# First attention of a two-layer block: keys on the partitions in place of turned probabilities

## The chip, the cores and the metric

The kernel runs on one core of one Trainium2 chip. The metric is the device time of one execution in microseconds; lower is better.

## The reference, cut to what matters

Two blocks run one after the other on 2048 tokens of width 1024. The change touches only the attention of the first, which has 4 heads, keys of 128 + 64 features (the 64 are rotated and shared by the heads) and values of 128:

```python
s = (jnp.einsum('bqhd,bkhd->bhqk', qn, k_nope)
     + jnp.einsum('bqhr,bkr->bhqk', qr, k_rope)).astype(jnp.float32) * scale
mask = pq[:, None, :, None] >= positions[:, None, None, :]
p = jax.nn.softmax(jnp.where(mask, s, neg), axis=-1)
return jnp.einsum('bhqk,bkhd->bqhd', p.astype(v.dtype), v)
```

The result times silu(gate_a), beside a pooling branch times silu(gate_b), goes through `w_out` and a layer norm. All is float32. Every query meets all 2048 keys; those after it are masked by position, not skipped.

## The kernel before

The first block works with features on the partitions and tokens as columns, in G = 4 groups of TB = 512 tokens. It begins with keys and values of all groups. Then each group g goes through three parts: the query tiles (`query_tiles`, L112: latents, gate_a, pool inputs, queries, gate_b, pool mix), the attention (`mla_steps`, L72) and the eight tiles of the out-projection (`("1out", g, c)`). The layer norm of group g - 1 runs inside the query tiles of group g. The second block follows, and the change leaves it as it is.

The order of the work is one list, `schedule()`. Each name in it is a PSUM tile; tiles go round RING = 6 banks. TensorE claims a tile after the reader of the tile six before has drained it (`claim`, L1845), and its readers wait with `wait_tile` (L699) and `wait_drained` (L702). Two more banks, `o_acc`, hold the value sums. Weight chunks of 512 KB pass through four slots in the order of the list (`stream_of`, L430): the queue of SP waits for a chunk's last tile and then loads the chunk four on. SP also loads the next group's x, before the weights of the first out-projection tile (L811 to L816). A project (L1853) is eight matmuls of 128 x 128 by 512 columns. A float32 matmul leaves two records in the trace, a transpose of 128 x 128 one.

The attention of a group works on units (`mla_units`, L67): two blocks of 128 queries of one head, eight units per group. In a unit TensorE computes scores with queries on the partitions: per block four tiles of 128 queries by 512 keys (k_nope, L1961), then the 64 rotated features (L1965), which use half the rows of the array, two matmuls side by side. VectorE drains each tile with `tensor_tensor_reduce` (L1397): it adds a bfloat16 mask made once per block (`mask_of`, L1344) and keeps the running maximum of each row. Two tiny instructions (L1406, L1407) give the negated maximum, and one instruction of ScalarE exponentiates 2048 columns with the maximum as bias and leaves the row sum (L1068). Now queries are on the partitions, and values need keys there. So TensorE turns the probabilities in blocks (L1977), ScalarE copies them out of PSUM (L1061), and TensorE multiplies values by them, 256 columns per matmul, into `o_acc` (L1987). The scores of the next unit are interleaved with the turns and values of this one. After every second unit VectorE takes the reciprocal of four sums, widens it (L1416), TensorE turns it (L1996), and VectorE multiplies it by gate and `o_acc` into `y_all` (L1422, L1426), on which the out-projection waits. GpSimd has no instruction in this part. Three buffers of probabilities rotate: two halves of `probs` and `lat` (L534).

Other lines that the steps touch: L1354 and L1355 normalise the query latents, L1379 multiplies the pooled branch by its gate, L1339 normalises key latents of 1024 columns, L880, L943, L944, L948 and L959 are GpSimd's, L1649 and L1650 VectorE's beside them in the second block, L1781 its drain of second-attention scores. L1890 makes keys.

Of the kernel before, what the change touches and what calls it, by code (L numbers as in the profile page):

```python
# [7 lines left out]
S = 2048  # L8
# [25 lines left out]
HUGE = 3e38  # L34

# [28 lines left out]
TILES_1 = S // TB  # L64


def mla_units(g):  # L67

    return [(BG * g + b, h) for b in range(0, BG, 2) for h in range(H1)]


def mla_steps(g):  # L72

    units = mla_units(g)

    def scores(u, e):
        return [("score", u, e), ("exp", u, e)] if u < len(units) else []

    yield from scores(0, 0) + scores(0, 1)
    for u, (i, h) in enumerate(units):  # L80
        first, second = scores(u + 1, 0), scores(u + 1, 1)
        yield from first[:1]
        yield from [("turn", u, c) for c in range(2)]
        yield from first[1:]
        yield ("value", u, 0)
        if h % 2 == 0 and u > 0:
            yield from [("share", u - 1), ("blend", u - 1)]
# [5 lines left out]
        if h % 2 == 1:  # L93
            yield ("sums", u)
        yield from [("value", u, c) for c in range(TILES_1 - 2, TILES_1)]
    yield from [("share", u), ("blend", u)]


def mla_tiles(g):

    units = mla_units(g)
    for st in mla_steps(g):
        i, h = units[st[1]]
        if st[0] == "score":
            yield from [("score", i + st[2], h, c) for c in range(TILES_1)]
        elif st[0] == "turn":
            yield from [("prob_t", i + e, h, st[2]) for e in range(2)]
        elif st[0] == "share":
            yield ("share1_t", i, h // 2)


def query_tiles(g):  # L112
# [10 lines left out]
    yield from [("gate_a", g, j) for j in range(2, 4)]  # L123
# [321 lines left out]
def program(nc, A, out_t):  # L445
# [10 lines left out]
    with ctx:  # L456
# [38 lines left out]
        mask = alloc(one, "mask", [P, 2, S], bf16)  # L495
# [38 lines left out]
        probs_1 = probs[:, 0:S], probs[:, S:2 * S], lat[:, :, :].rearrange("p j t -> p (j t)")  # L534
        turned_1 = [a.rearrange("p e t -> p (e t)") for a in (prob_t[:, 0:2, :], turns[:, :, :])]
# [39 lines left out]
        def y_of(g):  # L575
            return y_all

# [53 lines left out]
        row_max = sem("row_max")  # L631
# [85 lines left out]
        def half_units_before(g, u, e):  # L717

            return 2 * (len(mla_units(0)) * g + u) + e

        def blends_before(g, u):

            return (len(mla_units(0)) * g + u) // 2
# [69 lines left out]
        def _(sp):  # L793
# [8 lines left out]
            for name, arr, idx, _ in STREAM:  # L802
# [8 lines left out]
                if name[0] == "1out" and name[2] == 0 and name[1] + 1 < G:  # L811
                    if name[1] == 0:
                        wait_tile(sp, "krope", G - 1)
                    else:
                        sp.wait_ge(stored, 16 * name[1])
                    load_x(name[1] + 1, A["x_t"])  # L816
# [43 lines left out]
        def _(pool):  # L860
# [38 lines left out]
            for g in range(G):  # L899
# [20 lines left out]
                for j in range(4):  # L920
                    ins = pool.tensor_copy(halo[:, j, :], u_in[:, j, TB:TB + HALO])
                    step(pool, ins)
            pool.wait_ge(win_summed, 4 * G)
# [40 lines left out]
        def _(act):  # L964
# [61 lines left out]
            for g in range(G):  # L1026
# [7 lines left out]
                for j in range(4):  # L1034
# [14 lines left out]
                units = mla_units(g)  # L1049
                for st in mla_steps(g):  # L1050
                    kind, u = st[:2]
                    i, h = units[u]
                    if kind == "turn":
                        c = st[2]
                        m = (len(units) * g + u) * TILES_1 + c
                        to = turned_1[m % 2].rearrange("p (k e q) -> p k e q", k=BG, e=2)
                        for e in range(2):
                            wait_tile(act, "prob_t", i + e, h, c)
                            if m >= 2 and e == 0:
                                act.wait_ge(pv_done, m - 1)  # L1060
# [1293 lines left out]
```

## Time and profile before

| what | value |
|---|---|
| median of 3 runs | 3818.19 us (3817.41 to 3819.34) |
| the profiled execution | 3818.23 us |
| its span | 3816.4 us |
| mean granted TensorE clock | 0.964 of full speed |
| TensorE busy | 3511.4 us |
| VectorE, ScalarE, GpSimd busy | 1800.6, 1434.4, 415.0 us |

The span is the time from the first to the last record of the profiled execution. Busy times are sums over one engine's instructions, so engines that work side by side add to more than the span. The granted clock is 1.00 at 2.4 GHz and 0.50 at 1.2 GHz.

### The profile page before, as it was taken

To read this page: it belongs to the slowest core of one execution; us is meant where nothing else is said; L and a number is where in the kernel's file an instruction comes from. 1 tells how busy PE (TensorE), PEld (TensorE's weight loads), DVE (VectorE), ACT (ScalarE), POOL (GpSimd) and SP (SyncE) were. 2 spreads that over 40 slices of the span, in tenths; PEclk is the share of its full clock that TensorE was granted. 3 is DMA by queue.
4 is the path that set the end of the run, shared out by engine and by line. 5 is a ranking of instruction groups with operands and counts; after the bars stand their busy time and mean duration, and the time that the engine had idled before them with its cause. 6 is when DMAs were issued, how large, how long until landed. Compare 5 with 4: busy or idle time off the path is not lost.

```text
span 3816.4 us, 38713 instructions
## 1 busy us (share of the span) xinstructions
PE 3511.4 (92%) x14032; PEld 1921.9 (50%) x14032; DVE 1800.6 (47%) x4239; ACT 1434.4 (38%) x2445; POOL 415.0 (11%) x445
## 2 busy tenths in 40 slices
PE   8999999999999999999979989899897898787887
PEld 3445644564456446645545445654445643444653
DVE  3413322332232323234662577825778616878652
ACT  1213312341233114222331465515665515766551
POOL 0001011002100210011111201202011111010100
PEclk9999999999999999989989999899998999898999
DMA  4121013002300220041103121031110031110002
GB/s 175 55 83 39 1 61 121 12 1 72 121 1 6 77 89 1 28 149 63 60 9 113 61 67 37 23 99 55 61 42 1 23 113 44 47 53 1 1 8 82
DMA packets 71885, 205.55 MB, mean 54 GB/s; under 512 B 6376, under 2 KB 7952, under 8 KB 71440
## 3 DMA queue, kind: packets, MB, share of 16 engines
q1 hardware_dynamic: 63360, 187.32, 15.3%
q10 hardware_dynamic: 8336, 15.74, 1.1%
q8 instruction: 114, 1.87, 0.2%
q14 instruction: 75, 0.61, 0.0%
HBM read 185.46 MB, written 17.58 MB: 53 GB/s over the span
## 4 chain that ended last, share of the span: by engine, by line
PE 73%; DVE 12%; ACT 8%; issue 5%; DMA 1%; SPq 0%; POOL 0%; ACTq 0%; DVEq 0%; POOLq 0%
PE bank L1859 37%; PE bank L1961 6%; PE o_acc L1987 6%; PE bank L1965 3%; PE bank L1977 3%; PE bank L2199 3%; PE bank L2084 3%; PE bank L2211 2%; ACT prob_t L1123 2%; PE bank L2116 2%; PE o_acc L2225 2%; ACT pt_last L1123 1%; DVE rstd L1519 1%; PE bank L2065 1%; DVE tmp L1571 1%
## 5 line engine op out<-in xcount | busy, mean ns | idle before, releaser
L1859 PE MATMUL bank<-group_even,weights 128*128 128x512 f32 x1376 | 601.5, 595 | 17.1 <-DMA weights<-in_w_in_kv 11.7
L1859 PE MATMUL bank<-group_odd,weights 128*128 128x512 f32 x1376 | 607.8, 599 | 6.2 <-ACT tmp L1109 6.2
L1859 PE MATMUL bank<-y_all,weights 128*128 128x512 f32 x1024 | 441.6, 593 | 12.9 <-DVE y_all L1426 6.0
L1859 PEld LDWEIGHTS bank<-group_even,weights 128*128 128x128 f32 x1376 | 260.7, 191 | 337.0 <-issue 336.9
L1859 PEld LDWEIGHTS bank<-group_odd,weights 128*128 128x128 f32 x1376 | 262.9, 193 | 331.6 <-issue 331.3
L1859 PEld LDWEIGHTS bank<-y_all,weights 128*128 128x128 f32 x1024 | 193.9, 190 | 255.8 <-issue 241.1
L1397 DVE CUSTOM_DVE_ANT_0 probs<-bank,mask 128x512 f32<-128x512 f32 x172 | 108.5, 687 | 261.9 <-PE bank L1965 261.9
L1961 PE MATMUL bank<-k_nope,q_nope 128*128 128x512 f32 x512 | 231.1, 594 | 0.0
L2199 PE MATMUL bank<-kh,qa 64*128 64x512 f32 (+3 forms) x816 | 175.0, 501 | 31.0 <-DVE mx L1781 18.7
L1250 ACT ACTIVATE prob_t<-bank 128x512 f32<-128x512 f32 (+3 forms) x240 | 116.7, 535 | 148.6 <-PE bank L2211 148.3
L2225 PE MATMUL o_acc<-prob_t,v 128*64 128x128 f32 x1680 | 148.7, 285 | 11.1 <-ACT prob_t L1250 7.3
L1068 ACT ACTIVATE probs<-probs,stat 128x2048 f32<-128x2048 f32 x43 | 86.5, 2012 | 171.2 <-DVE stat L1407 171.2
L2225 PEld LDWEIGHTS o_acc<-prob_t,v 128*64 128x64 f32 x1680 | 120.7, 141 | 57.7 <-issue 40.9
L1961 PEld LDWEIGHTS bank<-k_nope,q_nope 128*128 128x128 f32 x512 | 94.4, 190 | 101.1 <-issue 99.8
L1315 DVE TENSOR_TENSOR tmp<-bank,turns 128x512 f32<-128x512 f32 x12 | 8.3, 692 | 252.7 <-PE bank L1859 249.8
L1965 PE MATMUL bank<-k_rope,q_rope 64*128 64x512 f32 x512 | 127.2, 615 | 0.0
L1987 PE MATMUL o_acc<-prob_t,val 128*128 128x256 f32 x512 | 126.3, 389 | 0.0
L2199 PEld LDWEIGHTS bank<-kh,qa 64*128 64x128 f32 x816 | 81.1, 197 | 88.5 <-issue 37.8
L1061 ACT ACTIVATE prob_t<-bank 128x512 f32<-128x512 f32 x128 | 70.1, 600 | 140.1 <-PE bank L1977 139.2
L1123 ACT ACTIVATE prob_t<-index,mids 128x384 bf16<-128x384 f32 (+2 forms) x72 | 64.7, 898 | 152.3 <-DVE mids L1592 142.5
L1987 PE MATMUL o_acc<-turns,val 128*128 128x256 f32 x512 | 121.0, 379 | 0.0
L730 DVE SCALAR_TENSOR_TENSOR group_even<-group_even,bank 128x512 f32<-128x512 f32 x32 | 22.0, 686 | 202.5 <-PE bank L1859 202.5
(386 smaller groups left out, 5564.2 us busy)
## 6 DMA issues: line engine op xcount, KB each, us to landing
weights<-in_w_in SPq DMA_DIRECT2D x101, 512.0 KB, 3.5
weights<-in_w_in_q SPq DMA_DIRECT2D x64, 512.0 KB, 3.5
weights<-in_w_out SPq DMA_DIRECT2D x64, 512.0 KB, 3.6
weights<-in_w_i SPq DMA_DIRECT2D x20, 512.0 KB, 3.5
group_even<-in_x_t SPq DMA_DIRECT2D x8, 1024.0 KB, 8.0
group_odd<-in_x_t SPq DMA_DIRECT2D x8, 1024.0 KB, 8.8
group_even<-x_t SPq DMA_DIRECT2D x8, 1024.0 KB, 8.3
group_odd<-x_t SPq DMA_DIRECT2D x8, 1024.0 KB, 7.2
```

The costliest lines, as they stand in the source:

```text
L1068: A_(p, p, ACT.Exp, scale=QK_DIM ** -0.5, bias=stat[:, 8 + n % 3:9 + n % 3], accum_out=stat[:, 16 + 2 * h + e:17 + 2 * h + e]).then_inc(pr ...
L1123: A_(tested_act[m % 2][:, 0:share], index_of(BG * g + b)[:, n - share:n], ACT.Sign, scale=-1.0, bias=mids[:, b, r:r + 1], accum_out=signs[ ...
L1250: drains(A_(prob_slots[2 * (m % 2) + e][:, 0:wide_], bank("p2_t", i, 2 * p + e, c)[:, 0:wide_], ACT.Copy), "p2_t", i, 2 * p + e, c)
L1397: drains(V.tensor_tensor_reduce(out=probs_1[n % 3][:, c * TB:(c + 1) * TB], in0=bank("score", i + e, h, c)[:], in1=mask[:, e, c * TB:(c + ...
L1859: ins = M(bank(*name)[:], ring[n % SLOTS][:, k * P:(k + 1) * P], rhs[:, k, :], start=(k == 0), stop=(k == chunks - 1))
L1961: M(bank("score", i + e, h, c)[:], q_nope[:, h, cols], k_nope[:, h, c * TB:(c + 1) * TB], start=True, stop=False)
L1965: M(bank("score", i + e, h, c)[:], q_rope[half, h, cols], k_rope[half, (c // 2) * TB:(c // 2 + 1) * TB], start=False, stop=True).then_inc( ...
L1977: ins = nc.tensor.transpose(bank(*name)[:, k * P:(k + 1) * P], probs_1[n % 3][:, at:at + P], ident[:])
L1987: ins = M(o_acc[h // 2][:, (h % 2) * 2 * P:(h % 2 + 1) * 2 * P], val[:, c * BG + k, h * P:(h + 1) * P], turned_1[m % 2][:, 2 * k * P:2 * ( ...
L2084: ins = M(bank(*st)[:], x_of(g)[:, k, b * P:(b + 1) * P], w[:, (k % 2) * TB:(k % 2 + 1) * TB], start=(k == 0), stop=(k == KC - 1))
L2199: ins = M(bank("s2", i, 2 * p + e, c)[:, at:at + end - first], qa[rows, p, (i % BG) * P:(i % BG + 1) * P], kh[rows, a, p, first:end], star ...
L2225: ins = M(o_acc[i % 2][e * DH2:(e + 1) * DH2, p * P:(p + 1) * P], v2[:, k, h * DH2:(h + 1) * DH2], prob_slots[2 * (m % 2) + e][:, (k % BG) ...
```

## The change

Scores come with keys on the partitions: the key block is the stationary operand and 512 queries stream past it. Their exponentials can be multiplied with values as they are, and nothing is turned but three rows of maxima and shares per head. A unit is now a head with all 512 queries, four per group; it has eight pairs of tiles, each tile 128 keys by 512 queries. A step s of `mla_steps` does the scores of pair s and the values of pair s - 10 (`LAG`).

- VectorE drains a score tile with one instruction: the minimum of the score and (query position + 0.5 - key position) times 2 to the 80.
- The maximum of a query is now over partitions. VectorE takes an elementwise running maximum of pairs, folds it, TensorE turns it (peak), VectorE reduces, ScalarE widens, TensorE turns it back (spread), ScalarE copies it to `peaks`.
- The peaks are subtracted from each pair in place, by GpSimd for pairs 2 and 5 of each head and by VectorE for the rest; ScalarE exponentiates pairs of 1024 columns.
- Sums over keys: GpSimd adds the pairs 0 to 6 of a head elementwise (0 to 3 in the last head of a group), VectorE the rest and the two parts together, during the steps of the head after the next (total); TensorE multiplies them with ones (sums), and a share is widened, turned and multiplied as before, once per head.
- Twelve slots of pairs rotate: `probs`, `lat`, `turns`, the buffer of the next x and a quarter of `y_all`. So the next x is loaded only after the first tile of the out-projection.
- The projections gate_a 2 and 3 move from the query tiles into the attention. gate_a 3 is copied raw, its silu follows near the end.
- Each out-projection tile takes the chunks 4 to 7 first, then 0 to 3, and its first tile waits for the last head only at chunk 3.

```diff
-        for c in range(2, TILES_1):
-            yield ("turn", u, c)
-            if c < TILES_1 - 1:
-                yield ("value", u, c - 1)
-        yield from second
+PAIRS_1 = NB // 2
+LAG = 10
+KEY_SLOTS = 12
+POOL_SHIFTS = (2, 5)
+def key_tiles(p):
+    a, j = p // BG, p % BG
+    return [(2 * a + e) * BG + j for e in range(2)]
+def sums_by_pool(u):
+    return 7 if u < H1 - 1 else 4
+def mla_steps(g):
+    total = H1 * PAIRS_1
+    for s in range(total):
+        u, p = s // PAIRS_1, s % PAIRS_1
+        yield ("score", s)
+        if s == PAIRS_1:
+            yield from [("peak", 0), ("gate_a", 2), ("spread", 0)]
+        elif u > 0 and p == 0:
+            yield ("peak", u - 1)
+        elif u > 1 and p == 1:
+            yield ("spread", u - 1)
+        if s >= LAG:
+            yield ("value", s - LAG)
+        if s >= LAG - 1:
+            yield ("shift", s - LAG + 1)
+        if u > 1 and p in (1, 2, 3):
+            yield ({1: "total", 2: "sums", 3: "share"}[p], u - 2)
+    u = H1 - 1
+    v = total - PAIRS_1
+    yield from [("shift", v - 1), ("value", v - 2), ("peak", u), ("value", v - 1), ("spread", u), ("total", u - 1), ("gate_a", 3),
+                ("sums", u - 1), ("shift", v), ("shift", v + 1), ("value", v)]
+    for n in range(v + 1, total):
+        if n + 1 < total:
+            yield ("shift", n + 1)
+        if n == v + 2:
+            yield ("share", u - 1)
+        if n == total - 1:
+            yield from [("total", u), ("sums", u)]
+        yield ("value", n)
+    yield ("share", u)
...
# SP: when the next x is loaded
-                if name[0] == "1out" and name[2] == 0 and name[1] + 1 < G:
+                if name[0] == "1out" and name[2] == SLOTS and name[1] + 1 < G:
...
# GpSimd
+                    if kind == "shift" and p in POOL_SHIFTS:
+                        pool.tensor_tensor(tiles, tiles, peaks[u % 2].unsqueeze(1).broadcast_to([P, 2, TB]),
+                                           ALU.subtract).then_inc(shifted_pool, 1)
+                    elif kind == "value" and p < sums_by_pool(u):
+                        pool.wait_ge(probs_made, pairs_before(g, n) + 1)
...
+                            sum_of(pool, pool.tensor_tensor(sum_pool, sum_pool, tiles[:, 0, :], ALU.add))
+                            pool.tensor_tensor(sum_pool, sum_pool, tiles[:, 1, :], ALU.add).then_inc(far_sum, 1)
...
# ScalarE
+                        A_(tiles, tiles, ACT.Exp, scale=QK_DIM ** -0.5).then_inc(probs_made, 1)
...
# VectorE
+                            drains(V.scalar_tensor_tensor(out=tiles[:, e, :], in0=query_pos, scalar=pos_q[:, t:t + 1],
+                                                          in1=bank("score", g, n, e)[:], op0=ALU.subtract, op1=ALU.min), "score", g, n, e)
...
+                            step(dve, V.tensor_tensor(lane_max2, lane_max2, tiles, ALU.max))
+                        if p == PAIRS_1 - 1:
+                            V.tensor_tensor(max_dve, lane_max2[:, 0, :], lane_max2[:, 1, :], ALU.max).then_inc(lane_max, 1)
...
+                        V.tensor_tensor(tiles, tiles, wide(peaks[u % 2], 2), ALU.subtract).then_inc(shifted, 1)
...
# TensorE
+                        for e, t in enumerate(key_tiles(p)):
+                            M(bank("score", g, n, e)[:], k_nope[:, h, t * P:(t + 1) * P], q_nope[:, h, :], start=True, stop=False)
+                        at = p * P
+                        for e in range(2):
+                            half = slice(e * ROPE, (e + 1) * ROPE)
+                            M(bank("score", g, n, e)[:], k_rope[half, at:at + P], q_rope[half, h, :],
+                              start=False, stop=True).then_inc(tile_ready, 1)
...
+                        pe.wait_ge(probs_made, pairs_before(g, n) + 1)
+                        for e, t in enumerate(key_tiles(p)):
+                            ins = M(o_acc[h % 2][:], val[:, t, h * P:(h + 1) * P], key_slot(g, n)[:, e, :],
+                                    start=(p == 0 and e == 0), stop=(p == PAIRS_1 - 1 and e == 1))
```

## Rows read from the trace of the kernel before

**Rows 1.** the page's busy time, share of the span and instructions.

```profile
PE 3511.4 (92%) x14032; PEld 1921.9 (50%) x14032; DVE 1800.6 (47%) x4239; ACT 1434.4 (38%) x2445; POOL 415.0 (11%) x445
```

**Rows 2.** busy time, clock and DMA by stretch: the first attention stage.

```profile
core 0: us, PE busy (x) PEld busy (x) DVE busy (x) ACT busy (x) POOL busy (x), PEclk, DMA share, GB/s
...
312.20:489.50 177.30, 175.40 (x786) 111.37 (x784) 58.81 (x182) 67.39 (x97) 0.00 (x0) 1.00 0.00 1
```

**Rows 3.** timeline of TensorE over one unit (start us, length us).

```profile
379.71 3.60 PE L1961 MATMUL bank<-k_nope,q_nope 128*128 128x512 f32 x8
...
388.72 3.60 PE L1961 MATMUL bank<-k_nope,q_nope 128*128 128x512 f32 x8
392.24 1.99 PE L1965 MATMUL bank<-k_rope,q_rope 64*128 64x512 f32 x8
394.16 1.97 PE L1977 MATMUL bank<-ident,probs 128*128 128x128 f32 x16
396.09 1.97 PE L1987 MATMUL o_acc<-prob_t,val 128*128 128x256 f32 x8
...
401.36 3.17 PE L1961 MATMUL bank<-k_nope,q_nope 128*128 128x512 f32 x7
```

**Rows 4.** query normalisation on VectorE and its reader on TensorE, group 1 (timeline).

```profile
584.92 2.29 DVE L1355 TENSOR_TENSOR lat<-lat,rstd 128x2048 f32<-128x2048 f32 x1
...
629.47 20.76 PE L1859 MATMUL bank<-lat,weights 128*128 128x512 f32 x48
```

**Rows 5.** groups on VectorE, 150 to 500 us (busy us, mean ns | idle).

```profile
L1397 DVE CUSTOM_DVE_ANT_0 probs<-bank,mask 128x512 f32<-128x512 f32 x44 | 27.8, 687 | 67.6 <-PE bank L1965 67.6
...
L1379 DVE SCALAR_TENSOR_TENSOR y_all<-bank,vec,y_all 128x512 f32<-128x512 f32 x4 | 3.0, 750 | 4.7 <-PE bank L1944 4.4
...
L1339 DVE TENSOR_TENSOR lat<-lat,rstd 128x1024 f32<-128x1024 f32 x1 | 1.2, 1225 | 0.0
```

**Rows 6.** groups on ScalarE from 300 to 500 us.

```profile
L1068 ACT ACTIVATE probs<-probs,stat 128x2048 f32<-128x2048 f32 x11 | 22.1, 2011 | 47.6 <-DVE stat L1407 47.6
L1061 ACT ACTIVATE prob_t<-bank 128x512 f32<-128x512 f32 x32 | 17.5, 598 | 35.0 <-PE bank L1977 34.8
```

**Rows 7.** timeline of VectorE, its start after the rope matmuls of rows 3.

```profile
393.54 0.69 DVE L1397 CUSTOM_DVE_ANT_0 lat<-bank,mask 128x512 f32<-128x512 f32 x1 [4.82 <-PE bank L1965]
```

**Rows 8.** GpSimd: seven additions in a chain (timeline), and 1024 columns (groups).

```profile
575.45 9.34 POOL L880 TENSOR_TENSOR probs<-probs 128x512 f32<-128x512 f32 x7 [0.42 <-ACT probs L1011]
...
L948 POOL TENSOR_TENSOR y_all<-probs 128x1024 f32<-128x1024 f32 x8 | 15.1, 1893 | 129.1 <-DVE probs L1650 129.1
```

**Rows 9.** GpSimd, VectorE in the second block (timelines from 3385 us); L943's group.

```profile
3385.48 1.42 POOL L943 TENSOR_TENSOR y_all<-probs 128x512 f32<-128x512 f32 x1 [7.62 <-DVE probs L1650]
3386.87 1.54 POOL L944 TENSOR_TENSOR y_all<-probs 128x512 f32<-128x512 f32 x1
...
3385.32 0.69 DVE L1649 TENSOR_TENSOR kh<-kh,probs 128x512 f32<-128x512 f32 x1
3386.04 1.41 DVE L1650 TENSOR_TENSOR kh<-kh,probs 128x512 f32<-128x512 f32 x1
...
L943 POOL TENSOR_TENSOR kh<-probs 128x512 f32<-128x512 f32 x24 | 24.9, 1039 | 75.5 <-DVE kh L1650 75.5
```

**Rows 10.** GpSimd and VectorE with a PSUM operand, from 2403 us (timelines).

```profile
2403.43 4.52 POOL L959 TENSOR_TENSOR group_odd<-bias,sel 128x256 f32<-128x256 f32 x7
...
2404.21 0.42 DVE L1781 CUSTOM_DVE_ANT_0 index<-bank,group_odd 128x256 f32<-128x256 f32 x1
```

**Rows 11.** TensorE at the end of the stage (timeline; in brackets idle time before).

```profile
489.46 11.00 PE L1859 MATMUL bank<-y_all,weights 128*128 128x512 f32 x25 [1.51 <-DVE y_all L1426]
```

**Rows 12.** TensorE after idle time (timeline); clock by stretch.

```profile
161.98 8.79 PE L1890 MATMUL bank<-lat,gate 128*128 128x512 f32 x16 [7.39 <-DVE lat L1339]
170.61 7.03 PE L1896 MATMUL bank<-gate,lat 128*128 128x512 f32 x16
...
154.00:162.00 8.00, 0.61 (x3) 0.02 (x1) 7.72 (x7) 0.69 (x1) 0.00 (x0) 0.78 0.16 61
```

More of the change, by code:

```diff
@@ L112, in query_tiles @@
+def mla_tiles(g):
+    for kind, n in mla_steps(g):
+        if kind == "score":
+            yield from [("score", g, n, e) for e in range(2)]
+        elif kind in ("peak", "spread", "sums", "share", "gate_a"):
+            yield ({"share": "share1_t", "sums": "sums1"}.get(kind, kind), g, n)
 def query_tiles(g):
@@ L122, in query_tiles @@
         yield ("1var", g - 1)
-    yield from [("gate_a", g, j) for j in range(2, 4)]
     yield from [("u", g, j) for j in range(4)]
@@ new lines, in widened @@
+                def widened(to, of):
+                    return A_(to.rearrange("p (b q) -> p b q", b=BG), of.unsqueeze(2).broadcast_to([P, BG, P]), ACT.Copy)
+                for kind, n in mla_steps(g):
+                    if kind == "peak":
+                        wait_drained(act, "peak", g, n)
+                        widened(tmp[:, 0, :], stat[:, 0:BG]).then_inc(peaks_wide, 1)
+                    elif kind == "spread":
+                        wait_tile(act, "spread", g, n)
+                        drains(A_(peaks[n % 2], bank("spread", g, n)[:], ACT.Copy), "spread", g, n)
+                    elif kind == "shift":
+                        u, p = n // PAIRS_1, n % PAIRS_1
+                        by_pool = units_before(g, u) * len(POOL_SHIFTS) + sum(q < p for q in POOL_SHIFTS)
+                        if p in POOL_SHIFTS:
+                            act.wait_ge(shifted_pool, by_pool + 1)
+                        else:
+                            act.wait_ge(shifted, pairs_before(g, n) - by_pool + 1)
+                        tiles = key_slot(g, n)
+                        A_(tiles, tiles, ACT.Exp, scale=QK_DIM ** -0.5).then_inc(probs_made, 1)
+                    elif kind == "gate_a":
+                        wait_tile(act, "gate_a", g, n)
+                        drains(A_(gate[:, n, :], bank("gate_a", g, n)[:], ACT.Silu if n < H1 - 1 else ACT.Copy), "gate_a", g, n)
+                    elif kind == "sums":
+                        if n == H1 - 1:
+                            wait_drained(act, "gate_a", g, n)
+                            A_(gate[:, n, :], gate[:, n, :], ACT.Silu).then_inc(gate1_made, 1)
+                        wait_drained(act, "sums1", g, n)
+                        widened(tmp[:, 1, :], stat[:, BG:2 * BG]).then_inc(shares1_made, 1)
@@ new lines, in _ @@
+                        for e in range(2):
+                            wait_drained(dve, "score", g, n, e)
+                        if p == 0:
+                            held_tiles = tiles
+                        elif p == 1:
+                            if units_before(g, u) > 0:
+                                before = units_before(g, u) - 1
+                                wait_tile(dve, "peak", before // H1, before % H1)
+                            step(dve, V.tensor_tensor(lane_max2, held_tiles, tiles, ALU.max))
+                        else:
+                            step(dve, V.tensor_tensor(lane_max2, lane_max2, tiles, ALU.max))
@@ L1928, in _ @@
                     variance_of("1", g - 1, sq_view(probs))
-                for j in range(2, 4):
-                    project(("gate_a", g, j), x_of(g), KC)
                 for j in range(4):
```

281 lines of the change are left out of this document (131 added, 150 removed).

## The prediction

> **What bounds the kernel now.** I read the engine summary first [rows 1]: TensorE is busy for 92% of the span and no other engine for half of it. Then the busy time by stretch [rows 2]: of each first-attention stage of 177.3 us (it comes four times, once per group of 512 queries) TensorE works 175.4 at a granted clock of 1.00, VectorE 58.8, ScalarE 67.4, GpSimd nothing. So the stage is TensorE's work in order, and any other engine has more than 100 us of room. TensorE's timeline [rows 3] gives that work for one unit (256 queries of one head): it starts at 379.71 and its successor at 401.36. Eight score tiles cost 2 x (3.53 + 1.92) = 10.9 us (start to start, 388.72 to 392.24 to 394.16). Sixteen of its 32 transposes take 1.93, so all take some 3.7, and 7.1 are left for the values. Eight units are 173.3 us, with four sets of share transposes and 1.9 us of idle time the 177.3. Per head and group (two units) that is 44.3 us. Only the transposes of probabilities, 8 x 3.7 = 29 us per stage, are work that another layout does without.
>
> **The change on TensorE.** A head of 512 queries now takes eight steps: two score tiles, then two value matmuls of the step ten back. Plain matmuls of 512 columns come at 0.43 us per record (48 in 20.76) [rows 4], 3.43 for eight where L1961 takes 3.53 before it changes to half rows [rows 3]. So two L1961 matmuls take 1.72 us and two value matmuls also 1.72. The rope pair is not halved in the same way. Before, four rope matmuls run two by two and take 1.92, of which 1.72 is streaming; 0.20 there and 0.10 at the end of L1961 are paid each time TensorE goes to half rows and back. Now it goes there for every pair: 1.72 + 0.10 + 0.86 + 0.20 = 2.88 per step instead of 2.73. A step is 2.88 + 1.72 = 4.60 us, 32 of them 147 us. Peak, spread and share turn four blocks each, 0.5 us at the 0.12 us per block of L1977 [rows 3]; the four one-column matmuls of sums are weight loads at best, eight records at that pace, 0.9. Together 2.4 per head, 9.5 per stage. gate_a 2 and 3 (sixteen records each, 2 x 6.87 us) move from the query tiles into the stage: TensorE's work is unchanged, and the cover they gave the query normalisation isn't needed, for L1355 ends at 587.2 and its reader starts at 629.5 [rows 4]. I therefore compare with 177.3 + 13.7 = 191.0. Pure TensorE work after is 147 + 9.5 + 13.7 = 170.5.
> The Trainium skill (TensorEngine Tiling (Array Packing), Key Properties) says that a change of tiling mode drains the engine; the trace agrees, with 0.30 us for a round trip. If switching cost nothing the step would be 4.30.
>
> **The new chain.** TensorE now waits in every step for something made a step ago. After the score pair of a step, VectorE drains two tiles (0.61 + 0.69, L1397's pitch and length [rows 5]), takes the maximum over 1024 columns (1.22, from L1339) and subtracts the peaks for the next pair (1.22); ScalarE then exponentiates 1024 columns, 1.07 between 0.60 for 512 and 2.01 for 2048 [rows 6]. VectorE starts 1.30 us after the rope matmuls start [rows 3, 7], 0.2 after TensorE could go on. With 0.15 for hand-overs that is 5.3 us from the end of a score pair to probabilities. TensorE wants them after 4.60. Since a late value also delays the next score, the pace is the mean of both, about 4.95.
> Two of eight subtractions are GpSimd's. It sits in an in-order queue behind the sum of the pair before, two additions of 1.26 to 1.35 (seven in 9.34) [rows 8]. Its 1024-column subtraction lies between 1.89 (L948, one operand a repeated column) and 2 x 1.26 = 2.52; I take 2.3.
>
> **VectorE and GpSimd together.** Before, GpSimd is idle in this stage. Where both run on SBUF operands later, the trace shows them excluding each other [rows 9]: GpSimd's L943 starts under L1649 and takes 1.42 instead of the 1.04 of its group; VectorE's L1650 starts under L943 and takes 1.41 instead of 0.69, ending 0.55 after L943 does; L944 in turn takes 1.54. An instruction of VectorE with one operand in PSUM doesn't show this: L1781 takes 0.42 beside L959, seven of which take 4.52 [rows 10]. So drains and share products are free; maxima, subtractions and sums are not. Per head VectorE spends 7 maxima and a fold (9.2), six subtractions (7.3) and two additions (1.4) that way, together 17.9; GpSimd 13 additions and two subtractions, 21. That is 39 us of 44: not a bound alone, but it lengthens the chain.
> The Trainium skill (SBUF — State Buffer, Who interferes with whom) has it as a rule: VectorE with two SBUF inputs and a GpSimd instruction that reads SBUF block each other wholly. The trace agrees, with the 1.41 us.
>
> **One head walked through**, time zero when its step 8u's score pair ends. Each engine in its order; who waits for the other gets the next turn, as in [rows 9]. Values can start at 1.2; 6.3 (after spread); 11.05; 16.55 (after sums); then GpSimd: sum of pair 1 until 19.1, VectorE's maximum until 20.3, subtraction for pair 2 until 22.6, exponential, 23.8, where TensorE was ready at 21.65. Then 28.4; 34.4 (ready 33.0, two additions got between VectorE's drain and its subtraction); pair 5 again GpSimd's, 36.85 to 38.1 the sum, until 40.45 the subtraction, 41.6 (ready 39.0); next head's step at 46.2. A head costs 46.2 us, where the two units cost 44.3. The 39.2 of pure work hold 7 us of waits.
>
> **A stage.** Ten score steps with peak, gate_a 2 and spread come before the first value. Eight scores take 23.0, the ninth until 25.9; the folded maximum is there at 26.6, peak, gate and spread end at 34.4, the tenth score at 37.3, and value 0 starts 5.3 later, at 42.6, with the eleventh score done at 40.2: 2.4 us of waiting. The rest of the first head's cycle brings the 17th score to 76.9, the 25th to 123.1, the last to 162.1. From there only values are left and chains lie bare: value 21 at 164.7; 22 at 170.5 (4.1 idle); peak, 23, spread, gate_a 3 and sums until 182.7. VectorE's subtraction for pair 24 stands behind the reciprocal of these sums, so value 24 starts at 185.4 (2.7 idle), 26 at 191.5 (2.2). GpSimd then has three sums of pairs, 25 to 27, before its subtraction for pair 29: additions until 202.3, subtraction 204.6, value 29 at 205.8 where TensorE was free at 196.6. VectorE's last sums end at 210.6, sums, value 31 and share at 213.8. The out-projection starts with the four chunks that don't need it, so the 1.5 us of idle before it [rows 11] goes. 213.8 - 191.0 = +22.8 per stage.
> **The clock.** In this stage it is 1.00 now. In the 8 us with the 7.4 us idle before L1890 its mean is 0.78, so it went to its lower level of 1.2 GHz, and the sixteen records that follow take 8.79 where the next sixteen take 7.03 [rows 12]. A 9 us wait in the tail will do the same, to two values, sums and first output tiles: +3 per stage, from 1.8 for one such fall and somewhat more for the order of small work.
> **Costed at nothing:** mask building goes (VectorE's, hidden); query_pos and the scaled positions are two short instructions beside TensorE's projections and mix. The load of the next x moves behind the first output tile, because its buffer holds keys; seven tiles of 6.87 us are left for it, 48 us. The next weights, queued on SP behind it, have three tiles, 20 us.
>
> **Sum.** 4 x (22.8 + 3) = +103 on 3818.2, the profiled execution's own time, which is the median as well: 3921, say 3920.
>
> **Rivals.** (A) The above, chance 0.55, own range 3885 to 3960: with L1379's 0.75 us for a drain with a column operand [rows 5] each step gains 0.1 to 0.15, with GpSimd at 1.89 two waits per head shrink by 0.4.
> (B) The two engines do not exclude each other in these forms; the waits for GpSimd's order remain. The same walk, without a wait of either for the other's instruction, has 5.3 us per chain and 0.6 and 1.3 us of waiting at pairs 2 and 5; it gives 41.9 per head and 193 per stage: +2, with the clock +3 to +5, 3826 to 3840, up to 3885 if they exclude each other in part. For it: GpSimd's operand of the subtraction is read twice and its form isn't in the trace. Against: [rows 9]. Chance 0.22.
> (C) Faster: TensorE stays the bound. The place is the wait of a value matmul for its exponential; the price is the 191.0 less TensorE's own work after: 170.5 + 2.5 for the first value is 18 us under 191, four times -72, 3746, and half the waits give 3780. It decides if probabilities are there less than 4.6 us after a score pair. For it: VectorE and ScalarE have little total work. Against: four operations in a row already sum to 5.3. Chance 0.18. (D) Longer waits than walked, because a queued GpSimd addition gets in front of both VectorE operations of every step: 50 us per head, +10 more per stage, over 3960. Chance 0.05.
>
> **Numbers.** 3920; 3800 to 3975 holds A, B, most of D and a third of C. What this kernel's runs can tell from no change is 0.2%, 7.6 us: faster 0.18, within 0.2% 0.04, slower 0.78 (A, D and nearly all of B).
>
> **What would show it.** Stage length near 214 with TensorE busy about 170 of it, VectorE's 1024-column operations in part at 2.0 to 2.6 us instead of 1.22, GpSimd's additions at 1.3 to 2.5, TensorE's idle time put down to ScalarE's exponential, the longest at pairs 2, 5, 22 and 29. A score step of 2.58 or GpSimd operations of unchanged length, with a stage under 190, would make this wrong.

## The result, and the profile after

The changed kernel takes 3924.35 us (median of four runs, 3921.61 to 3925.88), the kernel before 3818.6 in the same comparison: 1.0276 times as long (1.0259 to 1.0294), 106 us more. The profiled execution took 3923.1, with a span of 3921.2 and a mean granted clock of 0.954 (before 0.964). The forecast was 3920, in 3800 to 3975. That the total is within 5 us is luck: errors in its terms cancelled. They are taken apart below.

The page's busy times of the kernel after, beside [rows 1]:

```profile
PE 3487.0 (89%) x12752; PEld 1743.5 (44%) x12752; DVE 2172.0 (55%) x4124; ACT 1336.6 (34%) x2242; POOL 790.0 (20%) x661
```

TensorE works 24 us less in all and its span is 105 us longer. By stretch, the first attention stage of the kernel after, from its first score to the first record of the out-projection, and in it the eight steps from the 16th to the 24th score pair (columns as in [rows 2]):

```profile
299.68:516.17 216.49, 183.80 (x498) 72.80 (x497) 149.16 (x151) 44.96 (x49) 94.46 (x54) 0.94 0.02 5
370.18:416.59 46.41, 40.25 (x118) 16.01 (x117) 37.59 (x36) 10.20 (x11) 26.50 (x16) 1.00 0.00 1
```

The stage takes 216.5 us where 191.0 is what it replaces, and in the next groups 217.8, 216.4 and 218.3. The four are 105 us over 4 x 191.0, and 104.9 us lie between the two profiled executions, so the place of the loss is this stage. What the prediction costed at nothing (masks, the later loads of x and weights, the moved projections) did cost nothing: between the first two stages TensorE is busy without a gap before and after, and the stretch is shorter by the two projections that moved. By stretch, the kernel before and the kernel after:

```profile
489.46:680.97 191.51, 191.51 (x446) 84.84 (x447) 48.01 (x50) 31.49 (x47) 34.21 (x35) 1.00 0.30 96
...
516.17:693.84 177.67, 177.67 (x416) 78.66 (x415) 49.41 (x52) 29.04 (x44) 34.21 (x35) 1.00 0.30 98
```

In the first stage TensorE is idle for 32.7 us. What it waits for, in the waits of TensorE over the stage (total us, times, longest):

```profile
PE o_acc L2062 <- ACT lat L1123: 10.7, 5, 7.5
PE o_acc L2062 <- ACT probs L1123: 10.3, 5, 2.6
PE o_acc L2062 <- ACT group_odd L1123: 8.0, 5, 2.4
PE o_acc L2062 <- ACT turns L1123: 1.8, 2, 1.5
PE o_acc L2062 <- ACT y_all L1123: 1.0, 1, 1.0
PE bank L2034 <- DVE lanes L1468: 0.7, 1, 0.7
```

All but 0.7 us is a value matmul waiting for its exponential. In the timeline of TensorE in the kernel after, L2042 and L2046 are a score pair and L2062 two value matmuls:

```profile
407.24 1.98 PE L2062 MATMUL o_acc<-y_all,val 128*128 128x512 f32 x4 [0.96 <-ACT y_all L1123]
409.06 1.88 PE L2042 MATMUL bank<-q_nope,k_nope 128*128 128x512 f32 x4
410.87 1.13 PE L2046 MATMUL bank<-q_rope,k_rope 64*128 64x512 f32 x4
412.96 1.98 PE L2062 MATMUL o_acc<-probs,val 128*128 128x512 f32 x4 [0.96 <-ACT probs L1123]
...
419.91 3.62 PE L2062 MATMUL o_acc<-probs,val 128*128 128x512 f32 x4 [2.19 <-ACT probs L1123]
```

A step is 5.72 us (407.24 to 412.96), of which 0.96 is waiting; before pair 5, which GpSimd shifts, it is 6.95. The two engines that feed it, VectorE and GpSimd, in their timelines of the kernel after over the same steps:

```profile
406.37 1.41 DVE L1454 SCALAR_TENSOR_TENSOR group_odd<-prob_t,pos_q,bank 128x512 f32<-128x512 f32 x2 [0.28 <-PE bank L2046]
407.88 1.73 DVE L1466 TENSOR_TENSOR lanes<-lanes,group_odd 128x1024 f32<-128x1024 f32 x1
409.64 2.17 DVE L1478 TENSOR_TENSOR probs<-probs,prob_t 128x1024 f32<-128x1024 f32 x1
```

```profile
407.26 1.27 POOL L976 TENSOR_TENSOR lanes<-lanes,y_all 128x512 f32<-128x512 f32 x1 [2.25 <-ACT y_all L1123]
408.61 2.12 POOL L977 TENSOR_TENSOR lanes<-lanes,y_all 128x512 f32<-128x512 f32 x1
...
414.33 2.13 POOL L977 TENSOR_TENSOR lanes<-lanes,probs 128x512 f32<-128x512 f32 x1
416.42 2.35 POOL L964 TENSOR_TENSOR probs<-probs,prob_t 128x1024 f32<-128x1024 f32 x1
```

This is one step of mutual exclusion. GpSimd's first addition (407.26 to 408.53) runs beside the drains, which read PSUM, and takes 1.27. VectorE's maximum issues at 407.88, waits for it, and ends at 409.61. GpSimd's second addition issued at 408.61, waits for the maximum and ends at 410.73. VectorE's subtraction, issued at 409.64, waits for that and ends at 411.81. Each waiting operation ends about 1.1 us after the one it waited for (alone it takes 1.23 or 1.27), so its recorded length is that and what was left of the other's. The exponential then runs from 411.85 to 412.91, and the value matmul starts at 412.96.

### The profile page after: what moved, and what is told of

The parts are those of the page before. It is cut to its first block, busy times and chain, and to the rows that moved or that the text cites. A ratio compares the mean times of both kernels' runs of the same rounds, so it can differ in the third digit from the quotient of the medians.

```text
span 3921.2 us, 36159 instructions
## 1 busy us (share of the span) xinstructions
PE 3487.0 (89%) x12752; PEld 1743.5 (44%) x12752; DVE 2172.0 (55%) x4124; ACT 1336.6 (34%) x2242; POOL 790.0 (20%) x661
## 4 chain that ended last, share of the span: by engine, by line
PE 34%; DVE 10%; ACT 8%; issue 5%; POOL 1%; ACTq 0%; DVEq 0%; POOLq 0%
PE bank L1938 17%; PE bank L2283 3%; PE bank L2168 3%; PE bank L2295 2%; PE bank L2200 2%; PE o_acc L2309 2%; ACT prob_t L1186 2%; PE bank L2086 1%; ACT pt_last L1186 1%; PE bank L2149 1%; DVE rstd L1598 1%; DVE tmp L1650 1%; ACT index L1322 1%; ACT probs L1322 1%; DVE index L1860 0%
## 5 line engine op out<-in xcount | busy, mean ns | idle before, releaser
L2042 PE MATMUL bank<-q_nope,k_nope 128*128 128x512 f32 x512 | 249.0, 609 | 0.0
L998 POOL TENSOR_TENSOR y_all<-probs 128x512 f32<-128x512 f32 x32 | 34.3, 1071 | 718.0 <-DVE probs L1585 460.0
L2042 PEld LDWEIGHTS bank<-q_nope,k_nope 128*128 128x128 f32 x512 | 95.6, 195 | 129.0 <-issue 129.0
L2046 PE MATMUL bank<-q_rope,k_rope 64*128 64x512 f32 x512 | 144.5, 641 | 0.0
L2062 PE MATMUL o_acc<-probs,val 128*128 128x512 f32 x192 | 104.9, 681 | 42.4 <-ACT probs L1123 42.3
L765 DVE SCALAR_TENSOR_TENSOR group_odd<-group_odd,bank 128x512 f32<-128x512 f32 x32 | 22.0, 687 | 198.4 <-PE bank L1938 101.0
```

Source lines behind the costliest of these rows:

```text
L2042: M(bank("score", g, n, e)[:], k_nope[:, h, t * P:(t + 1) * P], q_nope[:, h, :], start=True, stop=False)
L2046: M(bank("score", g, n, e)[:], k_rope[half, at:at + P], q_rope[half, h, :], start=False, stop=True).then_inc(tile_ready, 1)
L2062: ins = M(o_acc[h % 2][:], val[:, t, h * P:(h + 1) * P], key_slot(g, n)[:, e, :], start=(p == 0 and e == 0), stop=(p == PAIRS_1 - 1 and e ...
```

## The experiments

Stage lengths are of the first group. The theory: the chain from a score pair to its exponential, lengthened by the exclusion and by GpSimd's queue, sets the pace of the steps, and a badly ordered tail adds to it. The rivals: the cost is mostly TensorE's own (half rows), or GpSimd's place in the chain alone. Comparisons with the kernel before on the same chip gave 3818.7 to 3819.6 for it.

**e1: GpSimd's sums write and do not read.** They become memsets, 2.1 us per pair where two unblocked additions take 2.5, and the sums of these pairs are left out. Its two subtractions per head stay.

```diff
-                            sum_of(pool, pool.tensor_tensor(sum_pool, sum_pool, tiles[:, 0, :], ALU.add))
-                            pool.tensor_tensor(sum_pool, sum_pool, tiles[:, 1, :], ALU.add).then_inc(far_sum, 1)
+                            for _ in range(3):
+                                sum_of(pool, pool.memset(sum_pool, 1.0))
+                            pool.memset(sum_pool, 1.0).then_inc(far_sum, 1)
```

> The changed kernel with GpSimd's additions of exponentials replaced by memsets of its sum tile, four per pair (two for pair 0), which take about as long and read nothing from SBUF; the sums of those pairs are left out. GpSimd's subtractions stay. Theory (the two engines exclude each other while both read SBUF, and that lengthens the chain from scores to exponentials): VectorE's 1024-column maxima and subtractions fall back to 1.22 us except beside GpSimd's two subtractions, a head falls from 48 us to about 42, the stage from 216 to about 198, the time to 3850 to 3870. Rival (only GpSimd's place in its queue matters): GpSimd is busy as long as before, so 3910 to 3925.

3850.67 us (1.0080, 1.0065 to 1.0095), 74 below the changed kernel. The stage takes 199.8, the eight steps 42.9. Groups of VectorE and GpSimd over the first group, e1:

```profile
L1468 DVE TENSOR_TENSOR lanes<-lanes,group_odd 128x1024 f32<-128x1024 f32 x7 | 8.6, 1226 | 0.7
...
L978 POOL MEMSET lanes<- 128x512 f32 x63 | 33.1, 525 | 43.8 <-ACT group_odd L1125 14.2 <-ACT probs L1125 14.0 <-ACT lat L1125 7.6
```

And the same group of maxima in the kernel after:

```profile
L1466 DVE TENSOR_TENSOR lanes<-lanes,group_odd 128x1024 f32<-128x1024 f32 x7 | 12.1, 1733 | 0.7
```

GpSimd is nearly as long at work per pair (4 x 0.53 us beside 2 x 1.27 unblocked), and these maxima are back at 1.23, though memsets run beside them: it is GpSimd's reading that blocks. Beside its subtractions, which still read, maxima stay long (two of them take 2.25 on average). Without the additions' reads, and with 0.4 us less per pair in GpSimd's queue, 74 of the 106 us are gone.

**e2: VectorE does all subtractions.** `POOL_SHIFTS = (2, 5)` becomes `()`.

> The changed kernel with no subtraction on GpSimd: VectorE does all eight pairs. Theory: the two long waits per head (pairs 2 and 5) become ordinary steps, 1.2 us less each, and the 7.5 us wait before value 29 in the tail goes, since it stood behind three sums on GpSimd; VectorE's ordinary steps stay blocked by additions at 5.7 us. Stage about 204, time 3865 to 3885. Rival (VectorE is the bound, and 2.4 us more of work per head cost that much): 3925 to 3935.

3907.71 us (1.0231, 1.0214 to 1.0248), 17 below. A miss: half of what was expected or less. The eight steps take 45.25 and the step at pair 5 is now like the others, 5.7 us. In the tail the 7.5 us wait is gone, and TensorE waits where it had not, in the timeline of e2:

```profile
505.52 1.54 PE L2069 MATMUL bank<-ones,lanes 128*128 128x1 f32 x8 [4.82 <-DVE lanes L1493]
```

VectorE's subtractions wait for GpSimd's additions there and end at 499.8; seven additions and a fold of VectorE follow, to 505.5, and the sums stand behind these.

**e3: values one step later**, so that two steps cover the chain.

```diff
-        if s >= LAG:
-            yield ("value", s - LAG)
+        if s >= LAG + 1:
+            yield ("value", s - LAG - 1)
...
-    yield from [("shift", v - 1), ("value", v - 2), ("peak", u), ("value", v - 1), ("spread", u), ("total", u - 1), ("gate_a", 3),
+    yield from [("shift", v - 1), ("value", v - 3), ("value", v - 2), ("peak", u), ("value", v - 1), ("spread", u), ("total", u - 1), ("gate_a", 3),
```

> The changed kernel with the value matmuls of a pair one more step after its subtraction (11 steps after its scores instead of 10), all else in place. Theory (TensorE waits for a chain of 5.3 to 7 us that has 4.6 us of cover, and no engine is full): with a second step of cover the waits in the steady part nearly vanish, a head falls from 48 to 41 to 42 us, the tail keeps its waits and gains a value pair, stage about 200 to 204, time 3860 to 3880. Rival (VectorE and GpSimd together are full, 39 us of exclusive time and 13 of VectorE's own): the head stays at 46 to 48 and the time within 10 us of 3924.

3869.78 us (1.0131, 1.0116 to 1.0146), 55 below. The steps took 44.5 and 41.0 us for a head instead of 46.4 and 47.5; the tail from the last score to the out-projection grew from 52.1 to 54.1.

**e4: half rows alone, in the kernel before.** Its scores go in two halves, two k_nope tiles and two rope tiles each, so TensorE goes to half rows twice as often.

```diff
-                        for c in range(TILES_1):
-                            claim("score", i + e, h, c)
...
-                        for c in range(TILES_1):
-                            half = slice((c % 2) * ROPE, (c % 2 + 1) * ROPE)
...
+                        for first in range(0, TILES_1, 2):
+                            for c in range(first, first + 2):
+                                claim("score", i + e, h, c)
...
+                            for c in range(first, first + 2):
+                                half = slice((c % 2) * ROPE, (c % 2 + 1) * ROPE)
```

> The kernel before, with its score tiles done in two halves: two k_nope matmuls and two rope matmuls, twice, so that TensorE changes to half rows and back twice as often; same work otherwise. Theory (a round trip costs 0.30 us): 64 more round trips in each of 4 stages less none, 16 per stage: +4.8 us per stage, +19 in all, 3837. Rival (the 0.30 us belong to the order of four tiles, not to the change): 3818.

3842.67 us (1.0062, 1.0047 to 1.0077): 24.0 us for 64 more round trips, 0.37 us each, where 19 us were expected. Timeline of TensorE, e4:

```profile
382.73 1.88 PE L1962 MATMUL bank<-k_nope,q_nope 128*128 128x512 f32 x4
384.55 1.13 PE L1966 MATMUL bank<-k_rope,q_rope 64*128 64x512 f32 x4
385.60 1.98 PE L1962 MATMUL bank<-k_nope,q_nope 128*128 128x512 f32 x4
387.52 1.13 PE L1966 MATMUL bank<-k_rope,q_rope 64*128 64x512 f32 x4
```

Four records of full rows followed by full rows take 1.72. Here they take 1.82 before half rows (382.73 to 384.55), and 1.92 between half rows (385.60 to 387.52): 0.10 more for the first matmul after the rope pair, which my working had missed.

**e5: e3 and e2 together**, and **e6: e5 with another tail.** e6's tail has the subtractions three ahead, two of them before and two behind VectorE's additions for the last head but one, and GpSimd adds three pairs of the last head in place of four:

```diff
-    return 7 if u < H1 - 1 else 4
+    return 7 if u < H1 - 1 else 3
...
-    yield from [("shift", v - 1), ("value", v - 3), ("value", v - 2), ("peak", u), ("value", v - 1), ("spread", u), ("total", u - 1), ("gate_a", 3),
-                ("sums", u - 1), ("shift", v), ("shift", v + 1), ("value", v)]
+    yield from [("shift", v - 1), ("value", v - 3), ("value", v - 2), ("peak", u), ("value", v - 1), ("spread", u),
+                ("shift", v), ("shift", v + 1), ("total", u - 1), ("shift", v + 2), ("shift", v + 3), ("gate_a", 3),
+                ("sums", u - 1), ("value", v)]
     for n in range(v + 1, total):
-        if n + 1 < total:
-            yield ("shift", n + 1)
+        if n + 3 < total:
+            yield ("shift", n + 3)
```

> The run e3 (values one step later) with no subtraction on GpSimd either. If chain and contention are two costs, the first now gone, the steady part is bound by VectorE with its blocked time: a head stays near 44.5 us; the tail's 7.7 us wait before value 29 shrinks to about 5. Time 3850 to 3865. If GpSimd's two subtractions were what bound the head in e3, it falls to 41 and the time to 3830 to 3840.

> As e5, and the tail of a stage in another order: the subtractions and exponentials of pairs 24 to 27 before gate_a 3 and the sums of head 2, each later one three pairs ahead of its value, and GpSimd sums three pairs of the last head instead of four. Theory (the tail's waits are order, not work: 54 us from the last score to the out-projection in e3, of which TensorE works about 40): the waits before value 24 and after value 27 go, 10 to 13 us per stage, time 3805 to 3825. Rival (VectorE and GpSimd are full in the tail too): 3845 to 3860.

3906.51 (1.0230, 1.0214 to 1.0245) and 3873.39 us (1.0141, 1.0125 to 1.0156). Both missed by far. e5 is 37 us over e3, from which only the engine of eight subtractions per stage differs, and its eight steps take 48.0 where e2's, with values earlier, take 45.25. The new tail gave 33. Timeline of TensorE, e5:

```profile
375.24 1.12 PE L2034 MATMUL bank<-ident,lanes 128*128 128x128 f32 x4 [5.06 <-DVE lanes L1468]
376.15 3.62 PE L2062 MATMUL o_acc<-lat,val 128*128 128x512 f32 x4
```

In place of e2's waits of about 1 us before most values, TensorE waits 5.06 us in one piece for VectorE's folded maximum, and the value behind it runs 3.62 us where 1.98 is full clock: the granted clock of these eight steps is 0.93, and 1.00 in e2's.

**e7: no sums on GpSimd, and VectorE does all subtractions.**

```diff
-                            sum_of(pool, pool.tensor_tensor(sum_pool, sum_pool, tiles[:, 0, :], ALU.add))
-                            pool.tensor_tensor(sum_pool, sum_pool, tiles[:, 1, :], ALU.add).then_inc(far_sum, 1)
+                            pool.memset(sum_pool[:, 0:8], 1.0).then_inc(far_sum, 1)
```

> The changed kernel with no subtraction on GpSimd and its sums left out (one memset per pair stands for them), values ten steps back as in the change. Nothing of GpSimd is left that reads SBUF in the stage, so this is the chain alone. Theory (two drains, maximum, subtraction, exponential in a row: 5.4 us against 4.7 of TensorE's): values wait 0.3 to 0.7 us in most steps, a head takes 41 to 42 us, the stage about 192, time 3815 to 3830. Rival (without contention the chain is covered): a head of 40, time below 3810.

3846.22 us (1.0069, 1.0053 to 1.0086); 16 over the expected range. The tail, in its old order, still has waits of 3.39, 2.61 and 2.58 us, and values there ran 3.5 us longer than at full clock. The eight steps take 41.4, as expected. Timeline of TensorE's value matmuls, e7:

```profile
401.15 1.98 PE L2061 MATMUL o_acc<-y_all,val 128*128 128x512 f32 x4 [0.46 <-ACT y_all L1122]
...
404.79 1.13 PE L2045 MATMUL bank<-q_rope,k_rope 64*128 64x512 f32 x4
405.93 1.98 PE L2061 MATMUL o_acc<-probs,val 128*128 128x512 f32 x4
...
411.15 1.98 PE L2061 MATMUL o_acc<-probs,val 128*128 128x512 f32 x4 [0.46 <-ACT probs L1122]
```

With GpSimd out of the way the chain is the prediction's bare one: the score pair that ends at 405.85 (1.06 after 404.79) has its value at 411.15, 5.3 us later. TensorE waits 0.46 us in every second step: 10.0 us for two steps, 5.0 each (4.95 was worked out).

**e8: e3 with e6's tail**, GpSimd keeping its two subtractions in the first three heads only (`pool_shifts(u)` gives none for the last).

> As e6, but GpSimd keeps its two subtractions in heads 0 to 2 (none in the last). Against e6 this tells which of the two is fuller: if VectorE is the bound (33 us of its own work and what blocks it), e8 is faster than e6 by 4 to 10 us; if their exclusive time is (a subtraction takes GpSimd 2.35 and VectorE 1.22), it is slower by as much. Either way 3805 to 3830.

3834.05 us (1.0039, 1.0026 to 1.0052), 39 under e6, though 4 to 10 were expected. The stage is 195.1. By stretch, one head of e8:

```profile
363.00:407.50 44.50, 39.98 (x118) 15.89 (x116) 42.94 (x40) 11.04 (x12) 30.24 (x17) 1.00 0.00 1
```

VectorE is at work or blocked in 42.9 of 44.5 us. Timeline of TensorE, e8, its longest wait there:

```profile
372.88 0.66 PE L2039 MATMUL bank<-ident,lanes 128*128 128x128 f32 x4 [2.67 <-DVE lanes L1473]
```

It waits for VectorE's folded maximum, and in this head for no exponential but once (0.95 us). With values later, the chain no longer sets the pace here; VectorE does, the fuller of the two engines, and giving it GpSimd's subtractions, as e5 and e6 do, costs 37 and 39 us. The head after takes 41.0.

**e9: the changed kernel with e8's tail only.**

> The changed kernel with only the tail of a stage reordered as in e8 (pairs 24 to 27 subtracted and exponentiated before gate_a 3, the rest three ahead of their values, no subtraction on GpSimd in the last head, three of its pairs summed there); values stay ten steps back. Theory (tail and steady part add up): it takes from 3924 what e8 took from e3, 36 us, 3885 to 3895. Rival (the tail's waits only matter once the values come late): above 3905.

3888.36 us (1.0181, 1.0166 to 1.0195): 36 below the changed kernel, as e8 is 36 below e3. From the last score to the out-projection it takes 45.0 instead of 52.1.

**e10: the maximum from PSUM.** VectorE writes the masked score back to its bank and takes the maximum there, tile by tile, with one operand in SBUF; ScalarE copies the bank out.

```diff
+                            ins = V.scalar_tensor_tensor(out=bank("score", g, n, e)[:], in0=query_pos, scalar=pos_q[:, t:t + 1],
+                                                         in1=bank("score", g, n, e)[:], op0=ALU.subtract, op1=ALU.min)
...
+                                ins = V.tensor_tensor(lane_max2[:, e, :], (held_tiles if p == 1 else lane_max2)[:, e, :],
+                                                      bank("score", g, n, e)[:], ALU.max)
...
+                            drains(A_(key_slot(g, n)[:, e, :], bank("score", g, n, e)[:], ACT.Copy), "score", g, n, e)
```

> The changed kernel with VectorE's masked score written back to PSUM, its maximum taken from there tile by tile (one SBUF operand, 2 x 0.69 us instead of 1.22), and ScalarE copying the masked tiles to SBUF. VectorE gets 0.2 us more work per step and 8.5 us per head less of the kind that excludes GpSimd. Theory (exclusion, not work, lengthens the steps of 5.7 us): blocked time per step falls from 1.5 to about 0.7, a head from 48 to 44 us, time 3870 to 3895. Rival (VectorE's work or ScalarE's place in the chain decides): 3925 to 3950.

3888.14 us (1.0181, 1.0164 to 1.0197), 36 below. The eight steps take 44.4. Timelines of GpSimd and of VectorE, e10, at the pair that GpSimd shifts:

```profile
410.56 1.27 POOL L978 TENSOR_TENSOR lanes<-lanes,probs 128x512 f32<-128x512 f32 x1
411.79 2.34 POOL L965 TENSOR_TENSOR probs<-probs,prob_t 128x1024 f32<-128x1024 f32 x1
```

```profile
409.58 0.69 DVE L1472 TENSOR_TENSOR lanes<-lanes,bank 128x512 f32<-128x512 f32 x1
410.19 0.75 DVE L1466 SCALAR_TENSOR_TENSOR bank<-prob_t,pos_q,bank 128x512 f32<-128x512 f32 x1
410.97 0.69 DVE L1472 TENSOR_TENSOR lanes<-lanes,bank 128x512 f32<-128x512 f32 x1
```

The maximum of 1024 columns has become two of 512, with one operand in PSUM: 0.69 each beside GpSimd's additions, which are 1.27 where the kernel after had 2.13 at this pair. TensorE's wait at this pair goes from 2.19 to 1.32.

**e11: e8 and e10 together.**

> e8 (values one step later, tail reordered) with the maximum from PSUM as in e10. In e8 VectorE is busy or blocked for 94% of the steady part and TensorE waits for it: a head takes 44.5 us, where TensorE's work is 40.0. Theory: with half of the exclusive time gone a head takes 41 to 42 us, three heads and four stages make 30 to 40 us less, 3795 to 3805, under both kernels. Rival (VectorE's own work, 34 us, and what stands between its instructions fill it anyway): 3830 or more.

3794.82 us (3793.82 to 3796.29; 0.9936, 0.9923 to 0.9949), 24 us faster than the kernel before. The three edits add up: 3924.35 - 55 (e3) - 36 (e9) - 36 (e10) = 3797. The same stretch as e8's above (here nearly a head and a step, for a head takes 40.5), e11:

```profile
363.00:407.50 44.50, 43.93 (x126) 17.39 (x128) 37.49 (x49) 20.44 (x30) 26.12 (x18) 1.00 0.00 1
```

TensorE works 43.9 of 44.5 us: in the steps it is the bound again. Of the stage's 186.1 us (183.5 in the second group) TensorE works 177.9 and is idle 8.1, and 6.2 of these are two waits of the tail, where 43.1 us pass from the last score to the out-projection.

## Why the prediction was right, and where its terms were not

**The mechanism (A) held.** Where they meet GpSimd's, VectorE's 1024-column operations take 1.7 to 2.3 instead of 1.22, GpSimd's additions up to 2.1 instead of 1.27, and TensorE's idle time stands against the exponential. e1 and e10 show the exclusion from both sides, by taking away GpSimd's reads and VectorE's second SBUF operand; e7 shows the bare chain: 5.3 us, as put, though its terms as written add to 5.2 (0.24 + 0.61 + 0.69 + 1.22 + 1.22 + 1.07 + 0.15). The Trainium skill (SBUF — State Buffer, Who interferes with whom) says that a VectorE instruction with two SBUF inputs contends with a GpSimd instruction that reads SBUF and not with one that only writes it; the traces agree, with 1.73 us beside additions and 1.23 beside memsets.

**The head** was predicted at 46.2. Eight steps take 46.4 and 47.5 in the two stretches used here, and 48.1 from the 17th score pair to the 25th, the walk's own stretch, of which 1.7 is two operations at the lower clock. The waits came where the walk had its long ones: first value 2.18 (2.4 predicted), pair 5 of a head 2.19 (2.6), pair 2 of a head 2.31, 1.54 and 1.47 (2.15). Between them the walk had one wait of 1.4, at pair 4; the rows have 0.96 at pair 3 and again at pair 4. GpSimd's subtraction, taken at 2.3 between 1.89 and 2.52, is 2.35 unblocked; at pair 2 of the second head it meets VectorE and takes 3.35.

**The stage** was put at 213.8 plus 3 for the clock, 216.8; it is 216.5. Three terms were mis-sized and cancel:

**TensorE's own work** was put at 170.5. The stage has 183.8 busy, of which 8.7 is the clock's (below), so 175.1. The mis-sized term is "0.20 there and 0.10 at the end of L1961" for half rows: a score pair comes every 2.97 us, not 2.88. In the timeline of TensorE, kernel after:

```profile
302.55 1.98 PE L2042 MATMUL bank<-q_nope,k_nope 128*128 128x512 f32 x4
304.46 1.13 PE L2046 MATMUL bank<-q_rope,k_rope 64*128 64x512 f32 x4
305.52 1.98 PE L2042 MATMUL bank<-q_nope,k_nope 128*128 128x512 f32 x4
```

That is 32 x 0.09 = 2.9 us of the 4.6; e4 prices the round trip at 0.37 independently. The rest I did not take apart.

**Waiting** was put at 213.8 - 170.5 = 43.3; it is 32.7. Half of the difference and more is the tail, where the walk had idle times of 4.1, 2.7, 2.2 and 9.2 us at values 22, 24, 26 and 29; they are 2.39, 2.61, none and 7.53. GpSimd was no faster than walked, as its timeline in the kernel after tells:

```profile
501.93 1.59 POOL L977 TENSOR_TENSOR lanes<-lanes,probs 128x512 f32<-128x512 f32 x1
503.48 2.34 POOL L964 TENSOR_TENSOR lat<-lat,prob_t 128x1024 f32<-128x1024 f32 x1
```

Its subtraction for pair 29 ends 206.1 us from the stage's start, where 204.6 was worked out. TensorE came to value 29 later, at 199.8 instead of 196.6, and so waited less: a part of the waiting I had counted was TensorE's longer work and its lower clock.

**The clock** was put at "+3 per stage", from one fall after the 9 us wait. Falls came behind waits of 2.2 to 2.6 us too. TensorE's timeline, kernel after, at the values of the first group that ran long (at full clock four records take 1.98 and eight 3.66):

```profile
354.86 3.43 PE L2062 MATMUL o_acc<-probs,val 128*128 128x512 f32 x4 [2.31 <-ACT probs L1123]
...
467.38 3.31 PE L2062 MATMUL o_acc<-group_odd,val 128*128 128x512 f32 x4 [2.19 <-ACT group_odd L1123]
...
487.92 5.37 PE L2062 MATMUL o_acc<-probs,val 128*128 128x512 f32 x8 [2.61 <-ACT probs L1123]
...
506.96 3.78 PE L2062 MATMUL o_acc<-lat,val 128*128 128x512 f32 x4 [7.53 <-ACT lat L1123]
510.53 2.75 PE L2062 MATMUL o_acc<-turns,val 128*128 128x512 f32 x4
```

With the one at 419.91 these are 8.7 us over their length at full clock; in e11 it is 2.9. No run changed the clock alone, and a value that runs long also gives the next chain time, so what the clock costs of the 106 us (at most four times 8.7, 35) is read from rows and not shown by an experiment.

So: +4.6, -10.6 and +5.7 us against my terms, together -0.3 in the first stage. Its path and its waits the prediction had; the closeness of the sum is chance.

**The rivals.** (B), no exclusion, would have given 41.9 per head and 193 per stage. e7, which has neither GpSimd's additions nor its place in the chain, has 41.4 and 196.7 and is still 0.7% slower than before: a bare chain with the tail as it was is enough for a loss, as (B) had it. (C), TensorE stays the bound, needs probabilities in less time than TensorE's own work covers; the changed kernel has four operations in a row behind every pair, and only e11, with two steps of cover and the contention halved, gets there. (D) happened in its mechanism and not in its price: GpSimd got in front of both VectorE operations in many steps, as seen above, but a head came to 48.1 at most in the first stage, not to 50.

**What I had wrong in the experiments** was VectorE. I took its two extra subtractions per head for a small burden. With them it is at work or blocked for 39.6 us of e2's eight steps of 45.25 and for 42.6 of e5's 48.0: e2 gained 17 us, and e5 and e6 lost 37 and 39 against the same kernels with GpSimd's subtractions. Of the 2.8 us by which e5's steps are longer than e2's, TensorE's own work, longer at the lower clock, is 1.8 (42.0 busy to 40.2); the rest I did not settle.

## What to carry to other kernels

When a stage is one engine's work in order, look at what each of its instructions will wait for after the change, not at how little the other engines do: a chain of four short operations on engines that were not full cost more here than the 29 us of transposes per stage that it replaced. Give such a chain two steps of cover (55 us here), and order the end of a stage, where cover runs out, by hand (36 us). Where VectorE and GpSimd share a stage, leave one operand of VectorE's operations in PSUM (36 us).

## What the runs showed of the hardware that I had not expected

- Waits of 2.2 us in otherwise full work can lower TensorE's clock, and need not. By stretch, kernel after, behind the wait that ends at 373.50 (2.19 us), and behind the one that ends at 419.91 (also 2.19 us):

```profile
373.50:377.50 4.00, 4.00 (x10) 1.74 (x12) 3.96 (x3) 0.00 (x0) 3.38 (x2) 1.00 0.00 0
...
420.00:422.00 2.00, 2.00 (x3) 0.92 (x4) 1.97 (x2) 0.00 (x0) 1.92 (x2) 0.53 0.00 0
```

  The first is at 2.4 GHz, the second nearly all at the lower level, 1.2. In the first stage four of the seven waits of 2.18 to 2.61 us have a value behind them that ran long. The rows don't tell what makes the difference.
- The first full-row matmul after half rows is itself 0.10 us late. The Trainium skill (TensorEngine Tiling (Array Packing), Key Properties) says that a change of mode drains the engine and gives no time for it; here the round trip is 0.37 us by e4's runs and 0.39 by the rows.
- A blocked VectorE instruction waits out GpSimd's whole instruction, so GpSimd's longest one sets the worst case. Timeline of VectorE, e8, where a maximum of 1.22 us met a GpSimd subtraction of 1024 columns:

```profile
385.19 3.38 DVE L1471 TENSOR_TENSOR lanes<-lanes,turns 128x1024 f32<-128x1024 f32 x1
```
